# Attention of the second block: two heads side by side, value products issued in turns

## The chip, the cores and the metric

The kernel runs on one core of one Trainium2 chip. The metric is the device time of one launch in microseconds (us), as the median of several executions. Before the change: median 2866.47 us of three runs (2864.66 to 2867.7).

## The reference, cut to what matters

The program is two transformer blocks of width 1024 over 1024 tokens. The change touches one part of the second block, the causal attention of eight heads. Query and key have 96 features (64 plain, 32 with a rotary position), the value has 64:

```python
def causal_block_attention(q, k, v):          # B=1, S=1024, H=8, dq=96, dv=64
    scale = dq ** -0.5
    def one_block(args):                      # blocks of 128 queries
        qblk, bi = args
        sc = jnp.einsum('bhqd,bkhd->bhqk', qblk, kf) * scale
        sc = jnp.where(kpos[None, :] <= qpos[:, None], sc, -jnp.inf)
        p = jax.nn.softmax(sc, axis=-1)
        return jnp.einsum('bhqk,bkhd->bqhd', p, vf)
```

The eight results of width 64 lie side by side in columns 512 to 1023 of the mixer's output, ahead of `w_out`. The mLSTM (matrix memory) of the same block fills columns 0 to 511; its stage comes right after the attention.

## The kernel before, in words

Each engine has one instruction stream, written out by hand; semaphores tie the streams together. The attention (`mla_pe`, `mla_act`, `mla_dve`, `mla_sp`, `mla_pool`) first makes queries, keys and values of all heads, and then runs a loop over 64 items `NQ[n] = (h, i)`: a head h and a block i of 128 queries. Item (h, i) has i + 1 key blocks of 128. For each item:

- `scores(n)` (line 2362, PE): queries times keys into `PS[n % 2]`, up to 512 columns in one product.
- The mask on the last block (line 2316), the row maximum (line 2318), its scaling (line 2320), all DVE; then the exponential with its row sum on ACT (line 2242) from `PS[n % 2]` to `x4[:, n % 2]`.
- `normalise(n)` on DVE: reciprocal (line 2307) and scaling of the row (line 2309), issued after the maximum of item n + 1.
- `turn(n)` (line 2372, PE): i + 1 transposes of 128x128 into `PS[2]`.
- `pt_copy(n)` (line 2265, ACT): the turned weights from `PS[2]` to one of two places, `x4[:, 2 + n % 2]`, issued after the exponential of item n + 1.
- `values(n)` (line 2384, PE): for each key block j a product whose stationary operand is `Vt[:, j, h, :]` (128 rows, 64 columns) and whose moving operand is the turned weight block (128 columns). It sums over j into `PS[3]`, partitions 0 to 63 for an even head and 64 to 127 for an odd one.

In PE's stream, pass n of the loop holds `scores(n + 2)`, `turn(n)`, `values(n - 1)`. When half of two heads' rows is complete, `mixa` (ACT, line 2275) and `mixa_low` (DVE, line 2280) split it into a high and a low part, `m2hi` and `m2lo`. From item 50 on, ACT and DVE also prepare the mLSTM inside the loop: `head_hi` (line 2446), `head_lo` (line 2456), `mask_dve` (line 2532), `log_weight_act` (line 2538). POOL waits for `pv_ready` 16 (two heads done) before it splits two weight tiles, and for 64 before the mLSTM's sums. SP loads rows for the mLSTM into places of `acc` that held the queries of heads 6 and 7, so it waits for their scores (`s_ready`).

Of the kernel before, what the change touches and what calls it, by code (L numbers as in the profile page):

```python
# [19 lines left out]
ACT = mybir.ActivationFunctionType  # L20
# [242 lines left out]
def two_block_kernel(nc, A, out):  # L263
# [34 lines left out]
    with ctx:  # L298
# [1883 lines left out]
        ROT, VTH = x4[:, 0, :], x4[:, 3, :]  # L2182
        QK_SCALE = 96.0 ** -0.5
        qT = acc
        NQ = [(h, i) for h in range(8) for i in range(C)]

        def q_bank(h):
            return PS[h % 2 * 2]
# [28 lines left out]
        def mla_act(act):  # L2217
            act.wait_ge(S["unit_done"], U_QKV)
            act.wait_ge(S["cs_moved"], 1)
            for h in range(8):  # L2220
                uq, uk = Step(U_QKV + 2 * h), Step(U_QKV + 2 * h + 1)
                if h == 3:
                    act.wait_ge(S["mq_stored"], 64)
                act.wait_ge(S["unit_done"], uq.times(1, 1))
                act.activation(qT[NOPE, h, :], q_bank(h)[NOPE, :], ACT.Copy).then_inc(S["q_copied"], 1)
                if h == 7:
                    act.activation(small[:, 44:45], ones[:, 0:1], ACT.Exp)
                act.wait_ge(S["unit_done"], uk.times(1, 1))
                act.activation(kT[NOPE, h, :], PS[uk.par][NOPE, :], ACT.Copy)
                if h:  # L2230
                    act.wait_ge(S["vh_t"], h)
                act.activation(VTH[RP, :], PS[uk.par][RP, :], ACT.Copy).then_inc(S["unit_out"][uk.par], 1)
                if h:
                    vt_act(act, h - 1)
            vt_act(act, 7)

            for n, (h, i) in enumerate(NQ):
                N = (i + 1) * P
                act.wait_ge(S["s_stat"], 2 * n + 2)
                if n >= 2:  # L2240
                    act.wait_ge(S["pt_ready"], n - 1)
                act.activation(x4[:, n % 2, 0:N], PS[n % 2][:, 0:N], ACT.Exp, bias=sm(n, 1), scale=QK_SCALE,
                               accum_out=sm(n, 2)).then_inc(S["p_ready"], 1)
                if n:
                    pt_copy(act, n - 1)
                if n > 1 and (n - 2) % 16 in (11, 15):
                    mixa(act, 2 * ((n - 2) // 16) + (n - 2) % 16 // 15)
                if 50 <= n < 58 and n % 4 in (2, 3):
                    head_hi(act, (n - 50) // 4, n % 2)
                if n >= 58 and n < 62:  # L2250
                    log_weight_act(act, n - 58)
            pt_copy(act, 63)
# [6 lines left out]
        def pt_copy(act, n):  # L2259

            N = (NQ[n][1] + 1) * P
            act.wait_ge(S["pt_ready"], n + 1)
            if n >= 2:
                act.wait_ge(S["pv_ready"], n - 1)
            act.activation(x4[:, 2 + n % 2, 0:N], PS[2][:, 0:N], ACT.Copy).then_inc(S["pt_out"], 1)

        def half_of(q):

# [2 lines left out]

        def mixa(act, q):
            k, t, bank = half_of(q)
            act.wait_ge(S["pv_ready"], 16 * (q // 2) + (12, 16)[q % 2])
            act.activation(m2hi[:, k, t], bank, ACT.Copy).then_inc(S["mixa_hi"], 1)

        def mixa_low(dve, q):
# [5 lines left out]
        def mla_dve(dve):  # L2283
            dve.wait_ge(S["unit_done"], U_QKV)
            dve.wait_ge(S["ang_step"], 11)
            dve.tensor_copy(ROT[RP, :], CS).then_inc(S["cs_moved"], 1)
            dve.wait_ge(S["cs_moved"], 1)
            for h in range(8):
                uq = Step(U_QKV + 2 * h)
                q = q_bank(h)  # L2290
                dve.wait_ge(S["unit_done"], uq.times(1, 1))
                if h:
                    dve.wait_ge(S["q_rope"], h)
                if h == 7:
                    dve.wait_ge(S["kr_copied"], 16)
                dve.tensor_tensor(qT[RO, h, :], q[RO, :], ROT[RO, :], ALU.mult).then_inc(S["q_a"], 1)
                dve.wait_ge(S["q_copied"], h + 1)
                dve.tensor_tensor(x4[RO, 1, :], q[SW, :], ROT[SW, :], ALU.mult).then_inc(S["unit_out"][uq.par], 1)
                dve.wait_ge(S["unit_out"][uq.par], uq.nth())
                dve.wait_ge(S["q_a"], h + 1)  # L2300
                dve.tensor_tensor(qT[RO, h, :], qT[RO, h, :], x4[RO, 1, :], ALU.add).then_inc(S["q_rope"], 1)

            def normalise(n):

                N = (NQ[n][1] + 1) * P
                dve.wait_ge(S["p_ready"], n + 1)
                dve.reciprocal(sm(n, 3), sm(n, 2)).then_inc(S["rs_inv"], 1)
                dve.wait_ge(S["rs_inv"], n + 1)
                dve.tensor_scalar(x4[:, n % 2, 0:N], x4[:, n % 2, 0:N], sm(n, 3), None, ALU.mult)\
                   .then_inc(S["p_norm"], 1)  # L2310

            for n, (h, i) in enumerate(NQ):
                N = (i + 1) * P
                dve.wait_ge(S["s_ready"], n + 1)
                late = PS[n % 2][:, N - P:N]
                dve.tensor_tensor(late, late, negm[:, :], ALU.add).then_inc(S["s_masked"], 1)
                dve.wait_ge(*count("s_masked", n + 1))
                dve.tensor_reduce(sm(n, 0), PS[n % 2][:, 0:N], AX.X, ALU.max).then_inc(S["s_stat"], 1)
                dve.wait_ge(S["s_stat"], 2 * n + 1)
                dve.tensor_scalar(sm(n, 1), sm(n, 0), -QK_SCALE, None, ALU.mult).then_inc(S["s_stat"], 1)  # L2320
                if n:
                    normalise(n - 1)
                if n > 2 and (n - 3) % 16 in (11, 15):
                    mixa_low(dve, 2 * ((n - 3) // 16) + (n - 3) % 16 // 15)
                if 54 <= n < 58:
                    mask_dve(dve, n - 54)
                if 52 <= n < 60 and n % 4 in (0, 1):
                    head_lo(dve, (n - 52) // 4, n % 2)
            normalise(63)

        def mla_pe(pe):
# [40 lines left out]
                    tr = pe.transpose(PS[2][:, j * P:(j + 1) * P], x4[:, n % 2, j * P:(j + 1) * P], ident[:, :])  # L2372
                tr.then_inc(S["pt_ready"], 1)

            def values(n):
                h, i = NQ[n]
                if n == 0:
                    pe.wait_ge(S["vh_tok"], 8)
                if n % 16 in (0, 4) and n > 4:
                    pe.wait_ge(S["mixa_lo"], 2 * (n // 16) - (1, 0)[n % 16 // 4])  # L2380
                pe.wait_ge(S["pt_out"], n + 1)
                o = PS[3][h % 2 * 64:h % 2 * 64 + 64, i * P:(i + 1) * P]
                for j in range(i + 1):
                    mm = pe.matmul(o, Vt[:, j, h, :], x4[:, 2 + n % 2, j * P:(j + 1) * P], start=(j == 0), stop=(j == i))  # L2384
                mm.then_inc(S["pv_ready"], 1)

            pe.wait_ge(S["unit_out"][par(U_QKV)], Step(U_QKV + 12).nth())
            pe.wait_ge(S["kr_copied"], 16)
# [5 lines left out]
            for n in range(64):  # L2394
                if n + 2 < 64:
                    scores(n + 2)
                turn(n)
                if n == 62:
                    weight_scores(pe, 0)
                if n == 63:  # L2400
                    turn_v(pe, 0)
                if n:
                    values(n - 1)
            values(63)

# [52 lines left out]
        def mlstm_sp(sp):  # L2460
            sp.wait_ge(S["mq_stored"], 64)
            for h in range(2):
                for i in range(2):
                    head_load(sp, h, i)
            sp.wait_ge(S["s_ready"], 32)
            sp.dma_start(vTm, proj2[4 * P:5 * P, :]).then_inc(S["mv_loaded"], 16)
            for n in range(NS):
                h, J = n // C, n % C
                if n in (4, 5):
                    sp.wait_ge(S["s_ready"], 8 * (n + 3))  # L2470
                if n >= ER:
                    sp.wait_ge(S["st_w"], n - ER + 1)
                sp.dma_start(erow[n % ER][:, J * P:T],
                             r_d[J * 4 + h:J * 4 + h + 1, J * P:T].to_broadcast([P, T - J * P]))\
                  .then_inc(S["r_bc_loaded"][n % ER], 16)
                if J == 3 and h < 3:
                    sp.wait_ge(S["mv_t"], h + 1)
                    sp.dma_start(vTm, proj2[(5 + h) * P:(6 + h) * P, :]).then_inc(S["mv_loaded"], 16)
                if n == 5:
                    sp.wait_ge(S["pv_ready"], 64)  # L2480
                if n in (7, 8, 15, 16):
                    if n == 15:
                        sp.wait_ge(S["qk_back"], 64 * 3)
                    head_load(sp, 2 + n // 15, (n - 7) % 8)
                if n in (6, 16, 24, 31):
                    om_sp(sp, (6, 16, 24, 31).index(n))
# [1484 lines left out]
```

## Time and profile before

| | |
|---|---|
| median of the runs | 2866.47 us (2864.66 to 2867.7) |
| span of the profiled execution | 2864.3 us, 32980 instructions |
| time of the profiled execution itself | not listed apart from its span; the span is 0.4 us below the lowest run |
| PE (matmul) busy | 2773.5 us, 97% of the span |
| DVE busy | 1814.7 us, 63% |
| ACT busy | 1021.8 us, 36% |
| POOL busy | 1277.5 us, 45% |
| attention loop, first scores to last value product | 1780.7 to 1977.7 us |

Engines: PE is the matrix engine (PEld its weight loads, which overlap its products), DVE the vector engine, ACT the scalar engine, POOL the third one, SP issues transfers. Busy time counts overlapping instructions once. A product's recorded duration includes its way through the array, so in a row of products the distance from start to start is shorter than one duration.

### The profile page before, as it was taken

The numbers are of one execution on the slowest core, as the hardware profiler recorded it, in microseconds if no ns is written. First come the engines' busy times: TensorE is split into PE (matmuls) and PEld (weight loads), VectorE is DVE, ScalarE is ACT, GpSimd is POOL, SyncE is SP. The second block draws the span as 40 slices with busy tenths as digits, with TensorE's granted clock in tenths as the row PEclk, the third lists the DMA queues.
The fourth block names the chain that finished last, engine by engine and source line by source line (L and its number), as shares of the span: only waits on it lengthen the run. The fifth ranks groups of instructions, "written<-read, shape, count | busy, mean of one in ns | idle before, by whom it ended". The sixth has DMA issues, their size and how long they took to land.

```text
span 2864.3 us, 32980 instructions
## 1 busy us (share of the span) xinstructions
PE 2773.5 (97%) x12578; PEld 2194.2 (77%) x12578; DVE 1814.7 (63%) x2070; ACT 1021.8 (36%) x1397; POOL 1277.5 (45%) x780
## 2 busy tenths in 40 slices
PE   7999999999999999999998999999998999999998
PEld 5888787877777888887786887666577688878777
DVE  3111354656748666678889667666637766777877
ACT  4000333333224333333443025455535433344444
POOL 2433222223436888883333433101322888833331
PEclk9999999999999999999999999999799999999999
DMA  5223232334342333337431534002343355565543
GB/s 178 95 95 120 73 125 81 127 101 155 125 147 74 110 107 100 111 120 236 158 118 37 197 115 124 1 32 87 103 133 103 107 151 162 169 206 162 161 134 132
DMA packets 336967, 348.90 MB, mean 122 GB/s; under 512 B 18915, under 2 KB 256602, under 8 KB 336822
## 3 DMA queue, kind: packets, MB, share of 16 engines
q1 hardware_dynamic: 327254, 311.30, 35.2%
q10 hardware_dynamic: 9568, 35.66, 3.1%
q8 instruction: 93, 1.52, 0.2%
q14 instruction: 52, 0.43, 0.0%
HBM read 237.53 MB, written 108.34 MB: 121 GB/s over the span
## 4 chain that ended last, share of the span: by engine, by line
PE 54%; DVE 9%; issue 2%; ACT 2%; DMA 1%; POOL 1%; DVEq 0%; SPq 0%; ACTq 0%; POOLq 0%
PE ps L3274 34%; PE ps L533 9%; PE ps L2362 2%; PE ps L2384 2%; DVE op_lo L3351 2%; PE ps L2732 1%; DVE sw_lo L3184 1%; PE ps L2372 1%; PE ps L2705 1%; PE ps L2850 1%; DVE acc L3595 1%; DVE acc L3602 0%; DVE acc L1889 0%; PE ps L2696 0%; PE ps L575 0%
## 5 line engine op out<-in xcount | busy, mean ns | idle before, releaser
L3274 PE MATMUL ps<-op_hi,sw_hi 128*128 128x512 f32 x1769 | 693.1, 392 | 16.9 <-DVE op_lo L3351 9.6
L3274 PE MATMUL ps<-op_hi,sw_lo 128*128 128x512 f32 x1769 | 689.9, 390 | 0.0
L3274 PE MATMUL ps<-op_lo,sw_hi 128*128 128x512 f32 x1769 | 689.6, 390 | 0.0
L499 POOL TENSOR_TENSOR w_hi_t<-w_raw,ones 128x1024 fp32r<-128x1024 f32 (+1 forms) x85 | 162.0, 1909 | 744.6 <-PE ps L533 356.5
L3274 PEld LDWEIGHTS ps<-op_hi,sw_hi 128*128 128x128 f32 x1769 | 332.9, 188 | 98.0 <-issue 18.1
L3274 PEld LDWEIGHTS ps<-op_hi,sw_lo 128*128 128x128 f32 x1769 | 332.6, 188 | 69.9
L3274 PEld LDWEIGHTS ps<-op_lo,sw_hi 128*128 128x128 f32 x1769 | 332.9, 188 | 68.7 <-issue 0.5
L656 DVE TENSOR_TENSOR stage<-ps,rstd 128x1024 f32<-128x1024 f32 x62 | 75.7, 1221 | 345.7 <-PE ps L533 327.2
L3174 ACT ACTIVATE sw_hi<-sw_sumNone 128x512 fp32r<-128x512 f32 (+1 forms) x252 | 157.1, 624 | 332.5 <-PE ps L3274 250.2
L533 PE MATMUL ps<-h1hi,w_hi_t 128*128 128x512 f32 x720 | 233.5, 405 | 12.9 <-DVE h1lo L617 8.9
L3184 POOL TENSOR_TENSOR sw_lo<-sw_sumNone,sw_hi 128x512 fp32r<-128x512 f32 x138 | 214.5, 1563 | 33.5 <-ACT sw_hi L3174 33.4
L533 PE MATMUL ps<-h1lo,w_hi_t 128*128 128x512 f32 x720 | 227.4, 397 | 0.0
L533 PE MATMUL ps<-h1hi,w_lo_t 128*128 128x512 f32 x720 | 227.2, 397 | 0.0
L503 POOL TENSOR_TENSOR w_lo_t<-w_raw,w_hi_t 128x1024 fp32r<-128x1024 f32 (+1 forms) x85 | 217.7, 2564 | 6.2
L3135 POOL TENSOR_TENSOR sw_sumNone<-sw_raw 128x512 f32<-128x512 f32 (+1 forms) x63 | 113.4, 1800 | 234.1 <-DVE sw_lo L3184 211.2
L3174 ACT ACTIVATE sw_hi<-sw_raw 128x512 fp32r<-128x512 f32 (+1 forms) x189 | 117.5, 622 | 199.5 <-PE ps L3274 197.7
L3184 POOL TENSOR_TENSOR sw_lo<-sw_raw,sw_hi 128x512 fp32r<-128x512 f32 x109 | 159.7, 1466 | 53.8 <-ACT sw_hi L3174 53.8
L533 PEld LDWEIGHTS ps<-h1hi,w_hi_t 128*128 128x128 f32 x720 | 133.8, 189 | 52.2 <-issue 10.5
L533 PEld LDWEIGHTS ps<-h1hi,w_lo_t 128*128 128x128 f32 x720 | 135.8, 189 | 33.3
L533 PEld LDWEIGHTS ps<-h1lo,w_hi_t 128*128 128x128 f32 x720 | 135.8, 189 | 33.3
L3150 POOL TENSOR_TENSOR sw_sumNone<-sw_raw,sw_sumNone 128x512 f32<-128x512 f32 (+1 forms) x63 | 91.3, 1449 | 87.5 <-DVE sw_lo L3184 84.8
L3142 POOL TENSOR_TENSOR sw_sumNone<-sw_sumNone,sw_raw 128x512 f32<-128x512 f32 (+1 forms) x63 | 98.7, 1567 | 62.9 <-DVE sw_lo L3184 60.2
(441 smaller groups left out, 4957.1 us busy)
## 6 DMA issues: line engine op xcount, KB each, us to landing
op_raw<-hidden SPq DMA_DIRECT2D x42, 1024.0 KB, 8.8
w_raw<-in_w_in SPq DMA_DIRECT2D x60, 512.0 KB, 4.0
sw_raw<-in_w_ffn_in SPq DMA_DIRECT2D x44, 512.0 KB, 5.4
proj<-stage ACTq DMA_DIRECT2D x42, 512.0 KB, 2.6
hidden<-hidden_blocks SPq DMA_DIRECT2D x13, 1536.0 KB, 6.2
acc<-proj SPq DMA_DIRECT2D x36, 512.0 KB, 4.5
hidden<-hidden_blocks SPq DMA_DIRECT2D x14, 1280.0 KB, 5.0
sw_raw<-in_w_up SPq DMA_DIRECT2D x32, 512.0 KB, 8.3
```

What stands on the lines that cost most here:

```text
L499: ins = pool.tensor_tensor(whi[:, u.par, s], raw[:, u.par, s], ones[:, 0:1].to_broadcast([P, n]), ALU.mult)
L503: ins = pool.tensor_tensor(wlo[:, u.par, s], raw[:, u.par, s], whi[:, u.par, s].bitcast(F32), ALU.subtract)
L533: mm = pe.matmul(out[:, b * HALF:(b + 1) * HALF], w, x[:, k, b * HALF:(b + 1) * HALF], start=(begin and k == ks[0] and n == 0), stop=(end ...
L656: dve.tensor_tensor(stage[:, u.par, :], PS[u.par if pair is None else pair][:, :], rstd[:, :], ALU.mult).then_inc(S["unit_out"][u.par], 1)
L2362: mm = pe.matmul(PS[n % 2][:, b:b + w], qT[0:96, h, i * P:(i + 1) * P], kT[0:96, h, b:b + w], start=True, stop=True)
L2384: mm = pe.matmul(o, Vt[:, j, h, :], x4[:, 2 + n % 2, j * P:(j + 1) * P], start=(j == 0), stop=(j == i))
L3135: pool.tensor_tensor(s1, a21, a22, ALU.add).then_inc(S["sw_sum"], 1)
L3142: pool.tensor_tensor(s2, s1, a11, ALU.subtract).then_inc(S["sw_sum"], 1)
L3150: pool.tensor_tensor(s2, a12, s2, ALU.subtract).then_inc(S["sw_sum"], 1)
L3174: act.activation(wshi[ring(m)][:, 0:n], weight_block(p, r), ACT.Copy).then_inc(S["sw_hi"], 1)
L3184: eng.tensor_tensor(wslo[ring(m)][:, 0:n], weight_block(p, r), wshi[ring(m)][:, 0:n].bitcast(F32), ALU.subtract).then_inc(S["sw_lo"], 1)
L3274: mm = pe.matmul(out, w, x[:, k, :], start=(k == 0 and i == 0 and r < 4), stop=(k == n - 1 and i == 2), skip_group_check=r >= 4)
```

## The change

Items are ordered by pairs of heads: (0,0), (1,0), (0,1), (1,1), and so on. The value products of the two heads of a pair are issued together, in turns for each key block j, the one head into partitions 0 to 63 of `PS[3]` and the other into 64 to 127. There are four places for turned weights in the place of two; the two new ones lie where `m2lo`'s first two tiles were. `values(m)` now stands for a pair; pass n of PE's loop issues `values(n // 2 - 1)` when n is odd. The passes of `mixa` and `mixa_low`, and the counts waited for, follow the new order. An SP transfer for the mLSTM waits for `s_ready` 63 where it waited for 56, since head 6 now ends at item 62.

```diff
-        NQ = [(h, i) for h in range(8) for i in range(C)]
+        NQ = [(2 * a + s, i) for a in range(4) for i in range(C) for s in range(2)]
+        turned_p = [x4[:, 2, :], x4[:, 3, :]] + [at(f"p_turned{n}", [P, T], kb)[:, :] for n, kb in ((2, 107.5), (3, 111.5))]
...
-                if n > 1 and (n - 2) % 16 in (11, 15):
-                    mixa(act, 2 * ((n - 2) // 16) + (n - 2) % 16 // 15)
+                if n % 16 == 11:
+                    mixa(act, 2 * (n // 16))
+                if n % 16 == 3 and n > 16:
+                    mixa(act, 2 * (n // 16) - 1)
...
             act.wait_ge(S["pt_ready"], n + 1)
-            if n >= 2:
-                act.wait_ge(S["pv_ready"], n - 1)
-            act.activation(x4[:, 2 + n % 2, 0:N], PS[2][:, 0:N], ACT.Copy).then_inc(S["pt_out"], 1)
+            if n >= 4:
+                act.wait_ge(S["pv_ready"], n - 3)
+            act.activation(turned_p[n % 4][:, 0:N], PS[2][:, 0:N], ACT.Copy).then_inc(S["pt_out"], 1)
...
-            act.wait_ge(S["pv_ready"], 16 * (q // 2) + (12, 16)[q % 2])
+            act.wait_ge(S["pv_ready"], 8 * (q + 1))
...
-                if n > 2 and (n - 3) % 16 in (11, 15):
-                    mixa_low(dve, 2 * ((n - 3) // 16) + (n - 3) % 16 // 15)
+                if n % 16 == 12:
+                    mixa_low(dve, 2 * (n // 16))
+                if n % 16 == 4 and n > 16:
+                    mixa_low(dve, 2 * (n // 16) - 1)
...
-            def values(n):
-                h, i = NQ[n]
-                if n == 0:
+            def values(m):
+                a, i = m // C, m % C
+                if m == 0:
                     pe.wait_ge(S["vh_tok"], 8)
-                if n % 16 in (0, 4) and n > 4:
-                    pe.wait_ge(S["mixa_lo"], 2 * (n // 16) - (1, 0)[n % 16 // 4])
-                pe.wait_ge(S["pt_out"], n + 1)
-                o = PS[3][h % 2 * 64:h % 2 * 64 + 64, i * P:(i + 1) * P]
+                if a and i in (0, 4):
+                    pe.wait_ge(S["mixa_lo"], 2 * a - (1, 0)[i // 4])
+                pe.wait_ge(S["pt_out"], 2 * m + 2)
                 for j in range(i + 1):
-                    mm = pe.matmul(o, Vt[:, j, h, :], x4[:, 2 + n % 2, j * P:(j + 1) * P], start=(j == 0), stop=(j == i))
-                mm.then_inc(S["pv_ready"], 1)
+                    for s in range(2):
+                        mm = pe.matmul(PS[3][64 * s:64 * s + 64, i * P:(i + 1) * P], Vt[:, j, 2 * a + s, :],
+                                       turned_p[(2 * m + s) % 4][:, j * P:(j + 1) * P], start=(j == 0), stop=(j == i))
+                        if j == i:
+                            mm.then_inc(S["pv_ready"], 1)
...
-                if n:
-                    values(n - 1)
-            values(63)
+                if n % 2 and n > 1:
+                    values(n // 2 - 1)
+            values(31)
...
-                    sp.wait_ge(S["s_ready"], 8 * (n + 3))
+                    sp.wait_ge(S["s_ready"], 59 + n)
```

## Rows read from the trace of the kernel before

**Rows 1.** Page, part 4: the chain that ended last, share of the span by engine.

```profile
PE 54%; DVE 9%; issue 2%; ACT 2%; DMA 1%; POOL 1%; DVEq 0%; SPq 0%; ACTq 0%; POOLq 0%
```

**Rows 2.** Windows: from, to, length; each engine's busy us (x instructions); clock, DMA, GB/s.

```profile
1780.00:1800.00 20.00, 17.41 (x53) 9.80 (x52) 11.28 (x30) 10.29 (x22) 0.00 (x0) 0.66 0.19 43
...
1805.93:1828.94 23.01, 22.69 (x133) 15.79 (x132) 14.91 (x42) 12.11 (x25) 0.00 (x0) 1.00 0.01 1
1828.94:1852.55 23.61, 22.73 (x134) 15.80 (x133) 15.64 (x42) 12.13 (x26) 10.67 (x16) 1.00 0.00 1
...
1921.60:1944.95 23.35, 22.89 (x136) 15.74 (x133) 17.50 (x46) 14.12 (x28) 0.00 (x0) 1.00 0.00 1
1944.95:1977.66 32.71, 31.65 (x203) 23.44 (x202) 20.82 (x51) 20.81 (x36) 0.00 (x0) 1.00 0.07 25
```

**Rows 3.** Waits from 1786 to 1980 us: who for whom, total us, times, longest.

```profile
ACT x L2265 <- PE ps L2372: 62.4, 59, 3.1
DVE ps L2316 <- PE ps L2362: 50.3, 42, 2.6
```

**Rows 4.** Timeline, three passes of the loop on PE: start, length in us, operation.

```profile
1832.12 0.70 PE L2362 MATMUL ps<-kT,acc 96*128 96x256 f32 x2
...
1832.66 1.04 PE L2372 MATMUL ps<-ident,x 128*128 128x128 f32 x8
...
1833.62 1.50 PEld L2384 LDWEIGHTS ps<-x,Vt 128*64 128x64 f32 x14 [0.17 <-issue]
1833.62 1.74 PE L2384 MATMUL ps<-x,Vt 128*64 128x128 f32 x14
...
1835.30 0.91 PE L2362 MATMUL ps<-kT,acc 96*128 96x384 f32 x2
...
1836.05 0.27 PE L2372 MATMUL ps<-ident,x 128*128 128x128 f32 x1
...
1836.25 1.96 PE L2384 MATMUL ps<-x,Vt 128*64 128x128 f32 x16
...
1838.14 1.13 PE L2362 MATMUL ps<-kT,acc 96*128 96x512 f32 x2
```

**Rows 5.** Timeline: the way from one item's scores to the turn before it.

```profile
1848.74 1.98 PE L2362 MATMUL ps<-kT,acc 96*128 96x512 f32 x4
...
1850.76 0.30 DVE L2316 TENSOR_TENSOR ps<-ps,negm 128x128 f32<-128x128 f32 x1 [1.14 <-PE ps L2362]
1851.10 1.22 DVE L2318 TENSOR_REDUCE small<-ps 128x1 f32<-128x1024 f32 x1
...
1852.61 0.69 DVE L2309 TENSOR_SCALAR x<-x,small 128x896 f32<-128x896 f32 x1
...
1853.36 0.98 PE L2372 MATMUL ps<-ident,x 128*128 128x128 f32 x7 [0.32 <-DVE x L2309]
...
1853.54 0.29 DVE L2318 TENSOR_REDUCE small<-ps 128x1 f32<-128x128 f32 x1
...
1854.13 0.75 DVE L2309 TENSOR_SCALAR x<-x,small 128x1024 f32<-128x1024 f32 x1
...
1857.51 0.29 DVE L2309 TENSOR_SCALAR x<-x,small 128x128 f32<-128x128 f32 x1
```

**Rows 6.** Lines 2384 and 1962: one product, ns least/median/most, first and last start.

```profile
L2384 PE MATMUL ps<-x,Vt x576: 272/273/476, 1788.6 to 1977.4; 128*64 128x128 f32 x192
...
L1962 PE MATMUL ps<-ident,acc x16: 197/198/220, 1644.0 to 1645.0; 4*128 4x4 f32 x16
```

**Rows 7.** Timeline: eight short products in a row (line 2340).

```profile
1758.37 0.71 PE L2340 MATMUL ps<-ident,x 64*128 64x64 f32 x8
```

**Rows 8.** Timeline: what DVE and ACT do for the mLSTM inside the loop.

```profile
1935.06 1.05 ACT L2446 ACTIVATE m2hi<-stage 128x1024 fp32r<-128x1024 f32 x1
...
1935.96 1.22 DVE L2456 SCALAR_TENSOR_TENSOR q_parts<-stage,q_parts 64x1024 fp32r<-64x1024 f32 x1
...
1942.64 0.28 DVE L2532 SCALAR_TENSOR_TENSOR ering<-maskb,ering 128x128 f32<-128x128 f32 x1
```

**Rows 9.** Timeline: the low part of one half of two heads' rows.

```profile
1872.55 0.69 DVE L2280 TENSOR_TENSOR m2lo<-ps,m2hi 128x512 fp32r<-128x512 f32 x1
```

## The prediction, made before the changed kernel was run

> **What bounds the kernel now.** The chain of waits comes first: PE holds most of it, DVE a small share [rows 1]. So the question is whether PE holds this stage too. The windows answer it. With the loop cut at every eighth item, one head takes 23.01 us, of which PE is busy 22.69 us and DVE only 14.91 us, at full clock [rows 2]. The other engines wait for PE and not the reverse: the copy of the turned weights waits 62.4 us in all for the transposes, the mask 50.3 us for the scores [rows 3]. The loop is bound by PE's stream, and what leaves it can be gained until the way through DVE and ACT becomes longer than the PE work that covers it.
>
> PE's time for a pair of heads can be rebuilt from start-to-start distances [rows 4, 5]. Scores cost 0.213 us per key block: the four products of the longest item take 1.98 us, less the 0.27 us that one product needs to pass the array, over 8 blocks. A transpose costs (1.04 - 0.27) / 7 = 0.110 us. A value product is two instructions, since the loop has 288 of them and the trace 576 [rows 6], and one instruction costs (1.96 - 0.27) / 15 = 0.113 us. A pair of heads has 72 blocks: scores 15.4, transposes 7.9, 144 value instructions 16.3 us. To each group comes a gap before it, read from one start to the next: 0.11 us from scores to transposes (1832.12 + 0.43 to 1832.66), 0.08 to values (1832.66 + 0.88 to 1833.62), 0.10 to the next scores (1833.62 + 1.58 to 1835.30), 0.29 per pass, 4.6 for sixteen. The sum is 44.2 us of the 46.0 that two heads take; 1.8 is waiting.
>
> **The change, part by part.**
>
> *Value products in turns.* Their number and shapes stay. What may change is the distance between them: neighbours now write different halves of the partitions with stationary operands of 64 columns each, so one may stream while the other does. No row of before has two neighbours of this kind, so the price is bounded. No overlap is 0.113 us each, and beyond it lies a cost for the change of half itself, a rival below. The lower end is half of 0.113, 0.057. Nearest to it are PE's shortest products: eight in 0.71 us with a duration of 0.22 are 0.070 us apart [rows 7], sixteen of a few columns start within 1.0 us, 0.067 apart [rows 6]. PE has issued nothing faster here, with a weight load to each as in this loop. I take 0.067. Per pair of heads that is 144 x 0.067 = 9.6 us for 16.3.
>
> The Trainium skill, "TensorE: Matmul & The Clock Gate", section on packing small matmuls, says that products in different column groups run at once, with 2.38 times the speed measured for three groups; two groups at a full factor of two would give the lower end above. The same section says that weight loads pass products in flight only when the row groups differ, and here both halves use all rows. The trace disagrees with that as it stands: fourteen loads of 1.50 us lie inside 1.74 us of products on the same rows [rows 4].
>
> *Fewer groups.* Eight value groups go and eight changes with them: per two passes the gaps are now 0.11 (transposes), 0.11 (scores), 0.11, 0.08 and 0.10, 0.51 us, 4.1 per pair of heads for 4.6.
>
> *Order of the items.* This is what the change pays. The turn of item n waits for its normalisation, which DVE does after mask and maximum of item n + 1. From the end of the scores of n + 1 to the turn of n the trace has 2.92 us: scores end at 1848.74 + 8 x 0.213 = 1850.44, mask at 1850.76, the turn at 1853.36 [rows 5]. Less the maximum (1.22) and the scaling (0.69), 1.01 us is fixed. The maximum takes 0.29 us for one block and 1.22 for eight, so 0.29 + 0.133 i; the scaling 0.29 to 0.75, so 0.29 + 0.066 i [rows 5]. What covers this on PE is the turn of n - 1, the value products if they stand between, and the scores of n + 2. Before, value products always stood between. Now only when n is even. For odd n the way is 1.01 + 0.29 + 0.133 (i + 1) + 0.29 + 0.066 i = 1.72 + 0.20 i. The cover is 0.110 (i + 1) + 0.213 (i + 2) and three gaps, 0.87 + 0.32 i. PE waits 0.86 - 0.124 i, 3.4 us over i = 0 to 6. For i = 7 the scores of n + 2 are those of the next pair's first block: 2.05 against 1.42, 0.6 us more. For even n the values cover it, except that `mixa_low` (0.69 us [rows 9]) falls on item 4 of a pair, where only one block of values stands between: 0.4 us. Together 4.4 us of waiting per pair of heads.
>
> Four places in the place of two let `pt_copy(n)` run when the values of n - 4 are done; PE issues these before the turn of n, so this wait adds nothing. If it did, the next exponential would be behind it in ACT's stream, and scores and turn behind that.
>
> *Sum for a pair of heads:* 15.4 + 7.9 + 9.6 + 4.1 + 4.4 = 41.4 us for 46.0, a gain of 4.6. With u for the distance of two value instructions it is 31.8 + 144 u, and the gain is zero at u = 0.099 us.
>
> *The last pair* also carries the mLSTM's preparation: four `head_lo` of 1.22 us and four masks of 0.28 on DVE, four `head_hi` of 1.05 on ACT [rows 8]. Before, PE covered it: the head that has most of it took 23.35 for 23.01 us [rows 2], and of the last 32.71 us PE was busy 31.65. Now it falls on items 50 to 57, the short blocks i = 1 to 4, where DVE is what the turn already waits for. Two `head_lo` at i = 2 are 2.4 us with no cover, the two at i = 4 with two masks about 2.2 after the slack of the even item, and `head_hi` at i = 1 and 3 about 1.2. I take 5.5 us, with 2 and 8 as the ends, so the last pair gains nothing: -4.6 + 5.5 = +0.9.
>
> *Moved or left at nothing.* The first pair begins while the granted clock is low (mean 0.66 of full speed from 1780 to 1800 us [rows 2]); its short items are now all at the start, where PE has less to do. Nothing to 2 us gained; I take nothing. POOL's split of two weight tiles still begins when two heads are done; it cost 23.61 - 23.01 = 0.6 us before [rows 2] and costs that again. Without this cover it would be the same 0.6. The two new places lie in latent tiles whose last reader is the projection of the queries, long done. The SP transfer that waits for `s_ready` 63 has the mLSTM's vector loads behind it in its queue, but these waited before for the end of all scores and values, so they come as early as the loop ends. The mLSTM after the loop only starts sooner. Its rows do not depend on anything that keeps the old time.
>
> *The whole:* three pairs at -4.6 and the last at +0.9 make -12.9 us. The span of 2864.3 us becomes 2851.4. The median of the runs shown lies 2.2 us above this span; with the same distance the changed kernel's median is 2853.6, rounded to 2854.
>
> **The rivals.**
>
> *The halves do not overlap.* If u stays at 0.113, a pair takes 31.8 + 16.3 = 48.1 us and less 0.3 for longer cover, 47.8: 1.8 us more than now. Three pairs are +5.4, the last about +4 as value products cover part of the preparation: 2876. For it speaks that no row shows an overlap between products; against it, that stationary operands of 64 columns leave half of the array's width free. It decides from u = 0.099. This is also the case in which the change does not do what it says.
>
> *A change of half costs like a change of group.* The gaps above are 0.08 to 0.11 us per change of kind. There are two changes of half per key block, 288 in all. At 0.09 us each that is 26 us more on top of the first rival: 2902. The skill's rule on row groups, named above, would work in this direction, by loads that no longer hide; the loads of before do hide in one half.
>
> *The order eats the gain.* Overlap comes, but only for every second neighbour, as a product and its second half share one place: one distance of 0.113 and one at the floor of 0.067 are 0.090 on average. The pair takes 44.8, three gain 3.6 us and the last loses 4: about 2867. Waits of 7 to 8 us per pair in the place of 4.4 give the same. So does a clock that falls at the short blocks of each pair: the first head, partly at low clock, had more than a head's usual time. For this speaks that the short blocks come in fours on end; against it, that PE kept the full clock through all later heads [rows 2].
>
> **How the numbers follow.** Overlap at 0.057 to 0.075: 0.65, with 2842 to 2862 as its own range (0.057 gains 4.3 more; the last pair's ends 2 and 8; the mLSTM's own low-clock stretches may fall 3 us otherwise). Gain eaten: 0.15, 2860 to 2870. No overlap: 0.14, 2870 to 2880. Costly changes: 0.06. The range 2842 to 2875 leaves out 0.05 below, and above it the costly changes and some two thirds of the no-overlap case. A difference under 0.2% (5.7 us) is about what a measurement of this kernel cannot tell from none. Faster by more: 0.63 (most of the first case and a little of the second). Within it: 0.18. Slower by more: 0.19 (0.13 of no overlap, 0.06 of costly changes).
>
> **What would show it.** The value group of the longest item pair, 32 instructions, should last about 0.27 + 31 x 0.067 = 2.3 us; 3.8 means no overlap, 6 costly changes. Idle time of PE before line 2372, ended by DVE's line 2309, should grow, mostly at every second turn of the short blocks. A pair of heads should take 41 to 42 us, the last one as long as before. The loop's last value product should end about 13 us earlier, and the rest keep its distances. If a pair took 46 us with short value groups, the chain through DVE would be the step that I got wrong; if the loop shrank and the total did not, the mLSTM's clock or transfers.

## The result and the profile after

The changed kernel has a median of 2838.7 us (five runs, 2838.16 to 2844.9), the kernel before on the same occasions 2864.66 (2859.08 to 2867.7). The ratio is 0.9925, with 0.991 to 0.9939 as its 95% interval: 0.75% faster, or 17 to 26 us. Set on the median that was known before, 2866.5 us, the ratio gives 2845 us. The forecast was 2854, with a range of 2842 to 2875. The two medians lie 26 us apart, at the upper end of that interval; taken from 2866.5 these would give 2840.5, below the range. So the range held only just, and the forecast gain of 13 us was too small by 9 to 13 us.

The windows of the two traces are cut at the same places: first scores of each pair of heads, last value product, last product of the mLSTM, end. Columns as in [rows 2]. First the kernel before:

```profile
1780.71:1828.94 48.23, 45.32 (x216) 28.95 (x214) 29.43 (x80) 24.31 (x51) 0.00 (x0) 0.86 0.07 15
1828.94:1875.56 46.62, 45.41 (x265) 31.59 (x265) 30.56 (x83) 24.25 (x51) 10.67 (x16) 1.00 0.01 3
1875.56:1921.77 46.21, 45.42 (x266) 31.60 (x265) 29.79 (x83) 24.24 (x51) 0.00 (x0) 1.00 0.13 47
1921.77:1977.66 55.89, 54.37 (x335) 39.17 (x334) 38.14 (x95) 34.92 (x63) 0.00 (x0) 1.00 0.04 15
1977.66:2079.62 101.96, 97.56 (x323) 58.67 (x323) 65.56 (x100) 53.26 (x69) 42.68 (x32) 0.80 0.41 126
2079.62:2864.30 784.68, 756.91 (x3396) 610.75 (x3395) 561.80 (x596) 334.29 (x472) 392.50 (x245) 0.99 0.47 148
```

Then the kernel after:

```profile
1779.78:1819.70 39.92, 35.47 (x197) 20.66 (x195) 29.70 (x81) 24.61 (x52) 0.00 (x0) 0.87 0.07 15
1819.70:1860.72 41.02, 35.99 (x266) 23.28 (x265) 30.24 (x83) 24.11 (x51) 10.57 (x16) 1.00 0.04 10
1860.72:1901.14 40.42, 35.98 (x267) 23.26 (x265) 29.24 (x83) 24.11 (x51) 0.00 (x0) 1.00 0.12 47
1901.14:1953.59 52.45, 44.07 (x355) 29.68 (x353) 37.09 (x94) 34.12 (x63) 0.00 (x0) 1.00 0.05 16
1953.59:2055.14 101.55, 94.70 (x323) 55.33 (x323) 64.91 (x100) 53.39 (x69) 42.77 (x32) 0.83 0.44 126
2055.14:2836.80 781.66, 755.30 (x3396) 609.67 (x3395) 561.86 (x596) 334.19 (x472) 392.77 (x245) 1.00 0.47 148
```

The loop went from 196.95 to 173.81 us, 23.1 less. Of the 27.5 us between the two spans, 0.9 lie ahead of the loop, 0.4 in the mLSTM and 3.0 behind it, where the clock's mean is 0.99 before and 1.00 after. So the spans differ by 4.4 us more than the loop does, and most of this lies behind the stage that was changed. PE is busy 36.0 of 40.4 us in a pair of heads where it was busy 45.4 of 46.2: it waits now. The chain of waits says the same (before: [rows 1]):

```profile
PE 51%; DVE 10%; issue 2%; ACT 2%; DMA 1%; POOL 1%; SPq 0%; DVEq 0%; ACTq 0%; POOLq 0%
```

The timeline of PE after, for one pair of heads from block 0 to block 2 (columns as in [rows 4]), shows what shrank and what grew:

```profile
1863.29 1.07 PE L2377 MATMUL ps<-ident,x 128*128 128x128 f32 x8 [0.98 <-ACT p_turned L2268]
1864.28 1.75 PE L2390 MATMUL ps<-x,Vt 128*64 128x128 f32 x28
1865.96 0.70 PE L2367 MATMUL ps<-kT,acc 96*128 96x256 f32 x2
1866.50 0.27 PE L2377 MATMUL ps<-ident,x 128*128 128x128 f32 x1
1866.61 0.59 PE L2367 MATMUL ps<-kT,acc 96*128 96x256 f32 x2
1868.10 0.33 PE L2377 MATMUL ps<-ident,x 128*128 128x128 f32 x1 [0.89 <-DVE x L2312]
1868.35 1.97 PE L2390 MATMUL ps<-p_turned,Vt 128*64 128x128 f32 x32
...
1871.22 0.81 PE L2367 MATMUL ps<-kT,acc 96*128 96x384 f32 x2
1872.80 0.44 PE L2377 MATMUL ps<-ident,x 128*128 128x128 f32 x2 [0.77 <-DVE x L2312]
```

The value group of 32 takes 1.97 us, so (1.97 - 0.27) / 31 = 0.055 us per instruction. Sixteen took 1.96 before [rows 4]. The second turn of each block waits for DVE's scaling (line 2312). The waits by name put the same in a sum: what PE's turns wait for DVE grew from 9.2 to 40.4 us, and DVE and ACT wait less for PE (before: [rows 3]; ACT's copies stand under two names now, 25.5 and 24.2 us). The weight loads stand for PE here, as they come first. Before, then after:

```profile
PEld ps L2372 <- DVE x L2309: 9.2, 19, 1.1
```

```profile
PEld ps L2377 <- DVE x L2312: 40.4, 38, 2.2
DVE ps L2319 <- PE ps L2367: 33.9, 28, 2.7
ACT p_turned L2268 <- PE ps L2377: 25.5, 29, 1.9
```

### The profile page after: what moved, and what is told of

Same layout as the page of the kernel before. It is cut to its first block, busy times and chain, and to the rows that moved or that the text cites. A ratio compares the mean times of both kernels' runs of the same rounds, so it can differ in the third digit from the quotient of the medians.

```text
span 2836.8 us, 32978 instructions
## 1 busy us (share of the span) xinstructions
PE 2729.4 (96%) x12578; PEld 2155.0 (76%) x12578; DVE 1814.4 (64%) x2070; ACT 1021.3 (36%) x1397; POOL 1277.9 (45%) x780
## 3 DMA queue, kind: packets, MB, share of 16 engines
q8 instruction: 93, 1.52, 0.2%
## 4 chain that ended last, share of the span: by engine, by line
PE 51%; DVE 10%; issue 2%; ACT 2%; DMA 1%; POOL 1%; SPq 0%; DVEq 0%; ACTq 0%; POOLq 0%
PE ps L3282 34%; PE ps L533 9%; DVE op_lo L3359 2%; PE ps L2367 1%; PE ps L2740 1%; DVE sw_lo L3192 1%; PE ps L2390 1%; DVE small L2321 1%; PE ps L2377 1%; DVE x L2312 1%; PE ps L2858 1%; DVE acc L3603 1%; DVE acc L3610 0%; PE ps L2713 0%; DVE acc L1889 0%
```

## The experiments

Each changes the changed kernel unless said otherwise. "Loop" is the time from first scores to last value product, with its four pairs of heads; ratios are to the kernel before on the same chip.

| run | loop, us | pairs, us | median, us | ratio (95%) |
|---|---|---|---|---|
| before | 196.95 | 48.2, 46.6, 46.2, 55.9 | 2864.7 | 1 |
| changed | 173.8 | 39.9, 41.0, 40.4, 52.5 | 2838.7 | 0.9925 (0.991 to 0.9939) |
| e1, head after head | 194.5 | 42.3, 45.9, 45.3, 61.0 | 2859.7 | 0.9993 (0.9983 to 1.0003) |
| e5, one half | 204.3 | 43.5, 48.6, 48.2, 64.1 | 2870.4 | 1.003 (1.0019 to 1.0042) |
| e2, turns of two | 176.6 | 40.0, 41.3, 40.7, 54.7 | 2843.6 | 0.9946 (0.9929 to 0.9962) |
| e3, before the turn | 168.1 | 37.4, 38.7, 37.7, 54.3 | 2832.2 | 0.9903 (0.9887 to 0.992) |
| e4, split | 166.6 | 37.9, 38.0, 37.6, 53.1 | 2830.8 | 0.9899 (0.9882 to 0.9915) |
| e6, two places | 170.6 | 37.0, 40.4, 39.2, 53.9 | 2838.3 | 0.9922 (0.9906 to 0.9939) |
| e7, low parts later | 171.9 | 39.8, 41.0, 40.4, 50.6 | 2836.7 | 0.9913 (0.9896 to 0.9929) |
| f3, split, both later | 162.4 | 37.9, 38.0, 37.6, 49.0 | 2827.8 | 0.9885 (0.9868 to 0.9901) |

**e1: head after head.**

```diff
-                for j in range(i + 1):
-                    for s in range(2):
+                for s in range(2):
+                    for j in range(i + 1):
```

> The changed kernel with one edit: in a group of value products all key blocks of the first head come before those of the second, so neighbours write the same half of the partitions but for one change per group. Order of items, four places and number of groups stay. Theory (neighbours of different halves stream at once, 0.055 us from start to start in the changed kernel against 0.113 before): the distance returns to about 0.113, the group of 32 lasts 3.8 us and not 1.97, a pair of heads takes some 8 us more (144 x 0.058), 33 us in all less what the longer cover saves, so 2866 to 2872 us, at or above the kernel before. Rival (the gain comes from the item order and from half as many groups): within 3 us of the changed kernel, 2836 to 2845.

The gain is gone: 2859.7 us, no difference from before that can be told. So it comes from the turns and not from order or fewer groups. The time is 6 us below the theory's band, as the distance did not return to 0.113: a group of 32 took 3.33 us, 0.099 each, and a group of eight was as short as with turns. The windows of 0.25 us over the group of 32, with that line's products alone (busy time, products on record, clock), show where:

```profile
1879.20:1879.45 0.25, 0.25 (x5) 1.00 0.00 0
1879.45:1879.70 0.25, 0.25 (x6) 1.00 0.00 0
1879.70:1879.95 0.25, 0.25 (x8) 1.00 0.00 0
1879.95:1880.20 0.25, 0.25 (x8) 1.00 0.00 0
1880.20:1880.45 0.25, 0.25 (x5) 1.00 0.00 0
```

In the middle, where the half changes, more products are under way, up to twice as many. Where two groups follow each other directly, at the end of e1's loop, the starts show it one by one. Here `x` holds the last products of the group of 28 (partitions 64 to 127), `p_turned` the first ones of the group of 32 (partitions 0 to 63), which stand behind them in the program:

```profile
1970.21 2.56 PE L2390 MATMUL ps<-x,Vt 128*64 128x128 f32 x25
1972.51 0.32 PE L2390 MATMUL ps<-p_turned,Vt 128*64 128x128 f32 x1
1972.61 0.27 PE L2390 MATMUL ps<-x,Vt 128*64 128x128 f32 x1
1972.67 0.27 PE L2390 MATMUL ps<-p_turned,Vt 128*64 128x128 f32 x1
...
1972.89 2.95 PE L2390 MATMUL ps<-p_turned,Vt 128*64 128x128 f32 x29
```

Three products of the later group start before the last one of the earlier group.

**e5: one half.** From e1, both heads to partitions 0 to 63.

```diff
-                        mm = pe.matmul(PS[3][64 * s:64 * s + 64, i * P:(i + 1) * P], Vt[:, j, 2 * a + s, :],
+                        mm = pe.matmul(PS[3][0:64, i * P:(i + 1) * P], Vt[:, j, 2 * a + s, :],
```

> The run with head after head, and both heads of a pair written to partitions 0 to 63 (the second head overwrites the first and the other half holds old values, so the attention's output is not computed; number and shapes of all instructions stay). It removes the last neighbours of different halves. The run with head after head still had groups of 32 in 3.33 us, 0.099 per instruction, as if some five instructions on either side of the change of half streamed together. Theory (only different halves overlap, over a few instructions around a change): 0.113 everywhere, the group of 32 lasts 3.77 us, a pair of heads takes 3.5 to 4 us more than with head after head, in all 2872 to 2878, clearly slower than the kernel before: this is what the new order costs without any overlap, the first rival of the prediction, which said 2876. Rival (the shorter groups came from something else, such as several heads' loads): 3.33 us stays and the time of the run with head after head, 2857 to 2862.

The theory held, 2 us below its band in the median (7 runs of 2864.65 to 2871.45): without any change of half every product costs 0.111 us, and the kernel is 0.3% slower than before. The groups of 32 and 8 in e5, then in e1:

```profile
1879.90 3.71 PE L2390 MATMUL ps<-p_turned,Vt 128*64 128x128 f32 x32
...
1890.47 1.09 PE L2390 MATMUL ps<-p_turned,Vt 128*64 128x128 f32 x8
```

```profile
1878.29 3.33 PE L2390 MATMUL ps<-p_turned,Vt 128*64 128x128 f32 x32
...
1888.32 0.67 PE L2390 MATMUL ps<-p_turned,Vt 128*64 128x128 f32 x8
```

One change of half saves 0.38 us in the long group and 0.42 in the short one, three to four distances of 0.111. If products started strictly in the order of the program, each half taking one at a time, a change could save only one distance. A group of twelve, six for each half, took 1.14 us in e1 for 1.52 in e5 and 0.88 in turns: past four of a kind the one change saves no more.

**e2: turns of two key blocks.**

```diff
-                for j in range(i + 1):
-                    for s in range(2):
+                for j0 in range(0, i + 1, 2):
+                    for s, j in [(s, j) for s in range(2) for j in range(j0, min(j0 + 2, i + 1))]:
```

> The changed kernel with the halves alternating every two key blocks (four instructions of the one head, four of the other). Theory A (starts stay in program order, one product streams per half, and the next in the stream starts when its own half is free): of eight instructions two changes overlap one slot each, six slots of 0.113 for eight, 0.085 us on average; a pair of heads +4.3 us, in all about +15, 2850 to 2858. Theory B (the engine looks far enough ahead to keep both halves busy): 0.055 stays, time as the changed kernel. Theory C (only one overlap per group matters): 0.11 and the time of the run with head after head.

Theory A fell, B held but for a trifle: 0.056 us, pairs two and three 0.2 to 0.3 us longer than in the changed kernel. The group of 32:

```profile
1867.39 2.02 PE L2390 MATMUL ps<-p_turned,Vt 128*64 128x128 f32 x32
```

Four instructions for one half in a row are still fully covered by four for the other; that is the reach that e1 showed. Its last pair is 2.2 us longer for another reason, the clock, told below.

**e3: the value group between scores and turn.**

```diff
                     scores(n + 2)
+                if n % 2 and n > 1:
+                    values(n // 2 - 1)
                 turn(n)
...
-                if n % 2 and n > 1:
-                    values(n // 2 - 1)
```

> The changed kernel with the value group of an odd pass issued between its scores and its turn and not behind the turn. Theory (a turn waits for DVE's mask, maximum and scaling, and pays when no value products stand between the scores of n + 1 and the turn of n): the odd turns are covered now and the even ones bare, where both items are of the same block; the waits move from odd to even and stay 4 to 6 us per pair of heads, total within 4 us of the changed kernel. Rival (the waits come from the copy of the turned weights, ACT, which now has the value products as cover before the next turn): waits fall by half, 8 to 10 us faster in all.

Both theories missed: the waits did not just move, and those that fell are DVE's and not the copy's (weight loads of turns behind DVE's scaling: 17.0 us for 40.4). The third pair of heads lost 2.7 us (37.7 for 40.4), the loop 5.7, and the median is 6.5 us below the changed kernel's. The two intervals overlap, so it is the pairs and the repeat below that carry this. What I had overlooked: the way to turn n starts at the end of the scores of n + 1. A group behind the turn of n - 1 covers only turn n. A group between the scores of n + 1 and the turn of n - 1 lies in the ways of both. The timeline at blocks 1 to 2, where the second turns had waited 0.77 and more:

```profile
1864.32 1.97 PE L2390 MATMUL ps<-p_turned,Vt 128*64 128x128 f32 x32
1866.21 0.33 PE L2377 MATMUL ps<-ident,x 128*128 128x128 f32 x1
1866.38 0.81 PE L2367 MATMUL ps<-kT,acc 96*128 96x384 f32 x2
1867.03 0.39 PE L2377 MATMUL ps<-ident,x 128*128 128x128 f32 x2
```

A repeat of this kernel, beside other runs. Its edit is that of e3; the low parts stay where they were, whatever its name says:

> Values between scores and turn, four places, as in the run of that name, measured again on this chip beside the others as their base. It is expected within 2 us of 37.4, 38.7, 37.7 and 54.3 us for its four pairs of heads, and at 0.990 of the kernel before.

It gave 2831.0 us and 0.9893 (0.9877 to 0.991), with pairs of 37.5, 38.7, 37.7 and 54.3 us: as expected.

**e4: the group split, half of it in each pass, between scores and turn.**

```diff
+                if n % 2 and n > 1:
+                    values(n // 2 - 1, 0)
+                if n % 2 == 0 and n > 2:
+                    values(n // 2 - 2, 1)
                 turn(n)
```

> The changed kernel with each value group cut in two halves of its key blocks, one issued in the odd pass and one in the next even pass, each between scores and turn, so that every turn has half a group as cover; the value products run one pass later. Theory of the bare turns: the 5 us of waits per pair of heads fall to 1 to 2, against 8 more changes of group at 0.2 us, so 2 to 3 us per pair, 8 to 14 in all: 2825 to 2832. Rival (DVE as a whole is the bound, 15.8 us of steps per head with its own gaps, twice that and 0.7 for two low parts per pair): no more than 1 us per pair, 2834 to 2840.

The middle pairs fell by 3.0 and 2.9 us as the theory said, 2830.8 us in all. But e3 had the same from moving the whole group, so the split itself is worth 0.1 to 0.6 us per pair at most.

**e6: two places.** From e3's idea, with two places and the group in the even pass; the copy of item n waits for the values of n - 2, as before the change.

```diff
+                if n % 2 == 0 and n:
+                    values(n // 2 - 1)
                 turn(n)
...
+            if n >= 2:
+                act.wait_ge(S["pv_ready"], n - 1)
+            act.activation(turned_p[n % 2][:, 0:N], PS[2][:, 0:N], ACT.Copy).then_inc(S["pt_out"], 1)
```

> The changed kernel with two places for turned weights in the place of four, as before the change; the value group of pair m is issued in pass 2m + 2 between scores and turn, the only place where two places suffice without a deadlock. Theory (the places themselves give nothing; what counts is that a group stands between scores and turn, where it covers this turn and the next): as the run with values before the turn, 37.5 to 39 us per pair of heads, 2828 to 2836. Rival (four places are what lets PE run ahead of ACT's copies): the copy of each second item is waited for, 1 us and more per group, 32 groups, 2860 or above.

It lies between: as fast as the changed kernel with half its places, 2.5 us of loop behind e3, and 2 us above its theory's band. The rival, 2860 or more, fell. The group now waits for ACT's copy:

```profile
1864.28 1.97 PE L2390 MATMUL ps<-x,Vt 128*64 128x128 f32 x32 [0.68 <-ACT x L2268]
```

The mLSTM's stretch is 97.2 us in e3 and 101.5 in e6, which is more of the difference in the total than the places.

**e7: the mLSTM's low parts at long blocks.**

```diff
-                if 52 <= n < 60 and n % 4 in (0, 1):
-                    head_lo(dve, (n - 52) // 4, n % 2)
+                if 58 <= n < 62:
+                    head_lo(dve, (n - 58) // 2, n % 2)
```

> The changed kernel with the four low parts for the mLSTM (DVE, 1.22 us each) at items 58 to 61 (i = 5 and 6) and not at 52, 53, 56, 57 (i = 2 and 4). Theory (in the short blocks nothing covers them): the last pair, 52.4 us from its first scores to the last value product, loses 2 to 3 us, 2836 or so beside the changed kernel's 2838.7 in the runs so far. Rival (DVE has as little slack at the long blocks, or ACT's high parts are what costs): within 1 us of it.

The last pair lost 1.8 us, 50.62 for 52.45, somewhat less than the 2 to 3 of the theory and more than the rival's 1; the total cannot tell it from the changed kernel. Its window, up to the end of the last value group, and that group:

```profile
1900.73:1951.35 50.62, 44.22 (x355) 29.60 (x353) 37.04 (x94) 34.56 (x63) 0.00 (x0) 1.00 0.05 16
```

```profile
1949.43 1.92 PE L2390 MATMUL ps<-p_turned,Vt 128*64 128x128 f32 x32
```

**f1, f2, f3: the parts that gained, together.** f1 is e3 with e7's edit, f2 also has ACT's high parts at items 54 to 57, f3 is e4 with both.

> Both edits that gained, together: the value group between scores and turn, and the low parts for the mLSTM at items 58 to 61. Theory (the two waits are different ones): the last pair's 54.3 us fall by 3, the other pairs stay at 37.4, 38.7 and 37.7; about 3 us less than with the group alone, 0.988 to 0.989 of the kernel before. Rival (a group between scores and turn already covers the low parts): 0.990 as with the group alone.

> As the run before it, and ACT's four high parts (1.05 us each) at items 54 to 57 (i = 3 and 4) and not at 50, 51, 54, 55 (i = 1 and 3). Theory (at i = 1 ACT's exponential with a high part in front is late for the scores after next): 1 to 2 us less in the last pair. Rival (ACT has room there): no difference beyond 1 us.

> The value groups cut in two, each half between scores and turn, with the low and the high parts later. The cut alone measured 0.9899 beside 0.9903 for the whole group between scores and turn. With preparation moved it should be within 2 us of the run with whole groups; it would be ahead by 1 us in the last pair (53.1 for 54.3 us before the move).

The last pair of heads took 52.7 us in f1 (54.3 in e3), 50.5 in f2 and 49.0 in f3. The medians were 2832.1, 2832.3 and 2827.8 us, the ratios 0.99 (0.9883 to 0.9917), 0.9896 (0.9876 to 0.9915) and 0.9885 (0.9868 to 0.9901). f3 has the shortest loop, 34.5 us less than before, and the lowest median of the study; its interval lies wholly below that of the changed kernel. f1 missed its theory: it won 1.6 us in the last pair and not 3, and nothing in the total, as its rival said. f2 won 2.2 us more there, with its theory, and again nothing in the total. f3's last pair is 1.5 us ahead of f2's and its median 4.5, more than the 2 that were expected. The rows of the mLSTM show where the time of the loop went in the profiled executions of e3, f1 and f2:

```profile
1948.71:2045.94 97.23, 88.10 (x324) 51.37 (x323) 64.11 (x100) 53.16 (x69) 42.66 (x32) 0.89 0.45 137
```

```profile
1947.23:2049.00 101.77, 94.57 (x323) 56.58 (x323) 65.60 (x100) 53.27 (x69) 42.70 (x32) 0.83 0.42 130
```

```profile
1945.30:2049.54 104.24, 97.78 (x323) 57.66 (x323) 65.32 (x100) 53.28 (x69) 42.76 (x32) 0.80 0.44 127
```

The same instructions take 97 to 104 us as the mean clock goes from 0.89 to 0.80, and 102.5 us in f3 (0.82). That a stage before ends 2 us earlier or later goes with other stretches of this one at the low level; the runs do not show what selects them. These executions were the shortest of four for e3 (2829.4 us) and the longest for f1 and f2 (2834.7, 2835.6). The clock also differs between executions of one kernel: f2 took 2827.0 and 2829.1 us with a mean of 0.987 over the whole, 2835.4 and 2835.6 with 0.984. So a few microseconds won in the loop can drown in a total.

## Why the prediction was right, and where its sizes were off

Sign and mechanism were right: the loop was bound by PE, the halves overlap, the new order takes part of it back. The size was not: the loop was to lose 12.9 us and lost 23.1, and nearly all errors point the same way, so it is by little that the total stayed in its range. By the prediction's own steps:

- **Value products in turns.** 0.067 us was taken, from the shortest products seen; it is 0.055. Over 576 instructions that is 6.9 us, the largest error. The lower end, half of 0.113, was the true one; the rows taken as a floor were other shapes with weight loads of 128 columns, and no floor for 64. The Trainium skill, "TensorE: Matmul & The Clock Gate", section on packing small matmuls, states that products in different tiles of the array run at once; the trace agrees, with 0.055 us for 0.111. The same section says that products start and end strictly in the order of the program. The trace does not agree: e1 has three products of a later group ahead of the last one of the group before, and a change of half saves three to four distances and not one.
- **Fewer groups, order of the items.** In the undisturbed third pair the waits ahead of turns sum to 5.2 us (predicted 4.4): 1.05, 0.95, 0.83, 0.42, 0.30, 0.58, 0.46, 0.34 and 0.22 us from the end of scores to the turn, less 0.11. They fall by 0.12 from block to block as the formula said, but for block 2, where two smaller ones stand. One is not DVE's: the last turn of the previous pair waits for ACT's copy. The gap from transposes to scores is 0 and not 0.11 us (1866.50 + 0.11 to 1866.61), those around values 0.14 and not 0.08 to 0.10. Without the value products' own gain a middle pair pays 2.7 us; 2.1 was predicted. Four pairs: 2.4 us against the forecast.
- **The last pair.** Its gain is 3.4 us in the place of 0.9 lost. Counted by the items issued up to the cut, it holds 204 value instructions after, 186 before, so 186 x 0.113 - 204 x 0.055 = 9.8 us were saved there and 6.4 paid: 2.7 as in other pairs and 3.7 for the preparation, within the ends 2 and 8; 5.5 was taken, 1.8 us too much. e7 removed 1.8 of the 3.7.
- **The first pair.** Taken at nothing beyond the rest, with 2 us as its end; it gained 8.3 us. Value products saved 102 x 0.113 - 84 x 0.055 = 6.9. The other 1.4 are a gain where a middle pair pays 2.7, so 4.1 us in favour. Two things are in it. The nearly equal means of the clock hide that the low level, half of full speed, lasted less: 2 x 0.14 x 48.2 = 13.5 us before and 2 x 0.13 x 39.9 = 10.4 us after, which is worth about 1.6 us where PE is busy. And turns that wait 0.83, 0.42 and 0.30 us in the third pair (the last of block 1 and both of block 2) wait for nothing here, as PE's own work in front of them takes longer at the low level:

```profile
1789.68 0.69 PE L2377 MATMUL ps<-ident,x 128*128 128x128 f32 x2
1795.15 0.53 PE L2377 MATMUL ps<-ident,x 128*128 128x128 f32 x3
```

  e5, with the order and no overlap, gains 4.7 us in this pair too (43.5 for 48.2). What made the low level shorter is not shown.
- **The sum.** -12.9 - 6.9 + 2.4 - 4.1 - 1.8 = -23.3, measured -23.1.
- **No overlap** as a rival was priced at 2876, 10 us above before; e5 measured 2870.4 beside 2861.2, 9 above, with 48.2 us for the third pair where 47.8 stood. The price of a middle pair was right. That the total was, is luck in part: the first pair gained 4.7 us where 1.8 of loss stood, and the last lost 8.2 where 4 stood. Without the overlap nothing of the gain is left.
- **The order eats the gain, by the clock.** It did not happen in the changed kernel (mean 1.00 in the last three pairs) but in its variants: most of them fell to the low level in the last pair (mean 0.94 in e1, e2 and e3, 0.90 in e4, 0.97 in e5, e6 and f1). The rows of e3:

```profile
1904.00:1908.00 4.00, 2.78 (x13) 1.18 (x13) 2.71 (x7) 3.71 (x8) 0.00 (x0) 1.00 0.00 0
1908.00:1912.00 4.00, 3.30 (x7) 1.33 (x7) 3.83 (x9) 1.68 (x6) 0.00 (x0) 0.59 0.00 0
1912.00:1916.00 4.00, 4.00 (x16) 1.98 (x15) 3.06 (x11) 1.84 (x4) 0.00 (x0) 0.56 0.00 0
```

PE had been busy 2.78 of 4 us before it fell. What it waited for there is ACT's exponential, late behind the mLSTM's high parts:

```profile
1906.02 0.91 PE L2367 MATMUL ps<-kT,acc 96*128 96x384 f32 x2 [0.90 <-ACT x L2243]
1908.30 1.70 PE L2367 MATMUL ps<-kT,acc 96*128 96x512 f32 x2 [0.62 <-ACT x L2243]
```

f1, with only the low parts moved, still fell; f2 and f3, with the high parts moved too, did not (mean 1.00). But such waits do not decide it alone. The changed kernel was less busy in two such stretches in a row and kept the full clock:

```profile
1912.00:1916.00 4.00, 2.38 (x10) 0.70 (x8) 3.80 (x9) 2.49 (x6) 0.00 (x0) 1.00 0.00 0
1916.00:1920.00 4.00, 1.93 (x10) 0.94 (x10) 3.83 (x12) 1.94 (x5) 0.00 (x0) 1.00 0.00 0
```

What selects the fall stays open. Its price shows in the last pair: the same 355 products on record keep PE busy 44.1 us in the changed kernel, 47.3 in e3 and 47.1 in e2. This is why e3's last pair (54.3 us) is longer than the changed kernel's in spite of shorter waits, and e2's by 2.2 us.

## What to carry to other kernels

Products with 64-column stationary operands cost half here when neighbours in the stream write different halves of the partitions; alternate at least every four instructions, the longest run that was seen fully covered. When an order is changed for that, write down for each waiting instruction which PE work stands between its trigger and itself: a group placed in front of a turn covered two of them, behind it only one, and that was worth 6 us of the loop here. Place the edits of other stages by the same list, and read the clock of the stretch beside each gain. A shape's price is bounded by rows of the same shape, not by the fastest other rows.

## What the runs showed of the hardware

- Two products of 128x64 on 128x128, to partitions 0 to 63 and 64 to 127, stream at once: 0.055 us per instruction for 0.111. Neighbours need not alternate strictly: runs of four per half (0.056) are as good, and one change of half in a group of 32 saves 0.38 us. Products to the two halves can start out of the order of the program (e1, 1972.51 to 1972.89 us).
- Weight loads of all rows did not hinder this: the same number of loads fits into 1.97 us that took 3.7 in e5.
- The clock fell to its low level (1.2 GHz) inside the attention loop in several variants, in e3 after a stretch in which PE waited for ACT (busy 2.78 of the 4 us before). The changed kernel kept the full clock through 2.38 and 1.93 of 4 us. The same products took 3 us more of PE's time where it fell.
- Over the whole program the mean clock differs between executions of one kernel, and the time with it: 2827.0 us at 0.987 and 2835.6 at 0.984 (f2).
